# A mixture-of-experts layer: expert outputs added to the residual rows in DRAM by indirect DMAs, in place of a one-hot combination on TensorE and a sum in SBUF

## The chip, the cores and the metric

The kernel is one program on one core of a Trainium2 chip. The metric is the device time of the whole program in microseconds (us); lower is better. Before the change it is 1360.62 us, the median of three executions (1358.38 to 1361.21). The trace comes from one further execution, which took 1361.19 us and whose span, from its first to its last instruction, is 1359.3 us.

## What is computed

One layer of a transformer is applied to 512 latent and 128 context tokens of width 1024, all in float32. The first half is a normalisation, an input projection, two kinds of attention, and an output projection, added to the residual. The change is in the second half, the expert layer:

```python
def expert_choice_ffn(h, w_router, w_gate, w_up, w_down):
    aff = softmax(h @ w_router)                      # per token, over 16 experts
    gates, idx = lax.top_k(swapaxes(aff, 1, 2), cap) # each expert picks its tokens
    xe = h[idx]
    a, u = xe @ w_gate, xe @ w_up                    # 1024 x 1024 per expert
    ye = (silu(a) * u) @ w_down * gates[..., None]
    return zeros.at[idx.reshape(-1)].add(ye)         # back to the rows of the tokens

h = rms_norm(x, g_ffn) * (1.0 + scale2) + shift2
x = x + gate2 * expert_choice_ffn(h, *moe_w)
y = rms_norm(x, g_final)
```

Each of the 16 experts picks 64 of the latent tokens and 16 of the context tokens, so 80 rows per expert. scale2, shift2 and gate2 are rows of 1024 numbers, one for latent tokens and one for context tokens. A token may be picked by several experts.

## The kernel before

The work is written out by hand for the five engines, which meet only at counted semaphores. Products are made to float32 accuracy by splitting each operand into a high part (rounded to fp32r) and a low part (the rest), and multiplying high by high, high by low, and low by high.

**Weights.** Each expert has three weight matrices (gate, up, down), each cut into 8 blocks of 128x1024 values, called halves here (512 KB). A group is 4 experts, so 96 halves; there are 4 groups, 384 halves. SP loads the halves into 12 slots in turn and may load a slot again once TensorE has used it (`s_half`). ACT rounds a half to `w_hi` (L1422, 6 buffers), DVE subtracts to get the low part (`expert_lo`, L1776), and TensorE runs `half_product` (L1078 to L1080): for each of two PSUM banks three matmuls of 128x512, six matmuls a half. ACT and DVE work 4 halves ahead (`LEAD`).

**Order.** `BLOCK_ORDER` sets it: g0 u0 g1 d0 u1 g2 d1 u2 g3 d2 u3 d3 for the experts 0 to 3 of a group, 8 halves each. Every engine's group body runs through the same 96 steps, `h`. Rows of the tokens are gathered for a whole group by one-hot matmuls (`gather`, L1028 and L1029) with `sel_g` and `sel_c`, the matrices that name the token of each slot; those for the next group are put between the halves of d3 (and `sel_g` for it is made at step 40). After u come the product h_act (L2023), four transposes a half of it (`turn_hidden`, L1069), and the split of the transposed values (`hidden_hi`, `hidden_lo`).

**Outputs, which the change replaces.** The result of a down projection stands in PSUM banks 4 and 5. ACT writes it times the gate of its row to `yc_f` for context rows (L1456) and to `ye_hi` for latent rows (L1458), and DVE writes the low part `ye_lo` (L2036). Two more one-hot matrices, `sel_t` and `sel_tc`, are made by DVE (`select_slots`) from the places and affinities of the tokens, which POOL brings by broadcasting DMAs from DRAM (L2260) in each group. When the four outputs of a group are there, TensorE adds them into token order (`combine`, L1049, L1050 and L1052): for each 128 tokens and each half of the 1024 columns four matmuls of 128x512 for latent tokens, and one in full float32 for context tokens. These ten steps of a group stand behind halves 5 to 14 of the next group; DVE adds each to `acc` in SBUF (L1976). Those of the last group stand behind everything, with the end of the program.

**The end.** In group 3 POOL reloads the residual rows `x_f` (2560 KB), gate2 (1024 KB) and `g_fin` from DRAM (L2285 to L2287). After the last half, for each of 5 tiles of 128 tokens: combine, two additions to `acc` (L1976), `acc` times gate2 (L2083), plus `x_f` (L2085), the sum of squares on ACT (L1495), the reciprocal root on POOL (L2130, L2133), times it and `g_fin` (L2088), and the store by POOL (L2300).

## Time and profile before

| | |
|---|---|
| time, median of 3 runs | 1360.62 us (1358.38 to 1361.21) |
| the profiled execution | 1361.19 us, span 1359.3 us |
| TensorE (PE) busy | 1223.0 us, 90% of the span |
| VectorE (DVE) busy | 972.2 us, 72% |
| ScalarE (ACT) busy | 751.3 us, 55% |
| GpSimd (POOL) busy | 136.5 us, 10% |
| mean granted clock of TensorE | 0.964 of full speed |
| moved by DMA | 295.26 MB |
| first expert half to the last | 692.66 us to 1314.32 us of the span |

PE is TensorE's matmuls and PEld its weight loads, which run beside them. A matmul's listed duration (some 0.39 us for 128x512) is longer than the distance from one start to the next, because matmuls are pipelined: what a matmul costs is the distance between starts. A wait is put down to the instruction that released it. The granted clock 1.00 is TensorE's upper level, 2.4 GHz; the lower is 1.2 GHz, in which starts lie 0.43 us apart.

### The profile page before, as it was taken

To read this page: it belongs to the slowest core of one execution; us is meant where nothing else is said; L and a number is where in the kernel's file an instruction comes from. 1 tells how busy PE (TensorE), PEld (TensorE's weight loads), DVE (VectorE), ACT (ScalarE), POOL (GpSimd) and SP (SyncE) were. 2 spreads that over 40 slices of the span, in tenths; PEclk is the share of its full clock that TensorE was granted. 3 is DMA by queue.
4 is the path that set the end of the run, shared out by engine and by line. 5 is a ranking of instruction groups with operands and counts; after the bars stand their busy time and mean duration, and the time that the engine had idled before them with its cause. 6 is when DMAs were issued, how large, how long until landed. Compare 5 with 4: busy or idle time off the path is not lost.

```text
span 1359.3 us, 17500 instructions
## 1 busy us (share of the span) xinstructions
PE 1223.0 (90%) x6001; PEld 966.1 (71%) x6001; DVE 972.2 (72%) x1245; ACT 751.3 (55%) x1049; POOL 136.5 (10%) x210
## 2 busy tenths in 40 slices
PE   2799977988889999999399999999999999999972
PEld 0578766767767777777288888788887888678851
DVE  1754528788756232444779999999999999799956
ACT  1523236666643221223568887588776887578831
POOL 2133330000000000000620001000010000100002
PEclk9899989999989999999699999999999999999976
DMA  9642231111053343554559997899888997999901
GB/s 327 263 174 69 62 89 30 30 30 30 1 217 124 124 124 127 214 203 155 201 205 382 369 368 228 305 389 366 308 296 294 383 363 266 379 339 375 369 35 77
DMA packets 109481, 295.26 MB, mean 217 GB/s; under 512 B 29857, under 2 KB 31602, under 8 KB 108642
## 3 DMA queue, kind: packets, MB, share of 16 engines
q1 hardware_dynamic: 102802, 265.99, 54.1%
q0 software_dynamic: 6032, 19.43, 4.3%
q10 hardware_dynamic: 576, 8.91, 1.7%
q8 instruction: 43, 0.70, 0.2%
q14 instruction: 28, 0.23, 0.0%
HBM read 276.78 MB, written 12.27 MB: 213 GB/s over the span
## 4 chain that ended last, share of the span: by engine, by line
PE 77%; DVE 11%; DMA 4%; ACT 3%; issue 3%; SPq 1%; POOL 1%; DVEq 0%; ACTq 0%; POOLq 0%
PE ps L1078 12%; PE ps L1079 12%; PE ps L1080 12%; PE ps L671 9%; PE ps L672 9%; PE ps L673 9%; PE ps L863 2%; DMA raw<-in_w_mod_dram 2%; PE ps L847 2%; DVE neg_max L1686 2%; DVE raw_lo L1776 2%; DMA raw<-in_w_exp_up_dram 1%; PE ps L886 1%; PE ps L693 1%; PE ps L1049 1%
## 5 line engine op out<-in xcount | busy, mean ns | idle before, releaser
L1776 DVE TENSOR_TENSOR raw_lo<-raw,w_hi 128x1024 fp32r<-128x1024 f32 x256 | 300.9, 1217 | 33.1 <-ACT w_hi L1422 26.4
L1422 ACT ACTIVATE w_hi<-raw 128x1024 fp32r<-128x1024 f32 x252 | 259.2, 1057 | 62.0 <-PE ps L1080 58.5
L1078 PE MATMUL ps<-w_hi,xe_hi 128*128 128x512 f32 x512 | 207.6, 405 | 1.8 <-DVE xe_lo L1950 1.8
L1080 PE MATMUL ps<-w_hi,xe_lo 128*128 128x512 f32 x512 | 201.8, 394 | 0.0
L1422 ACT ACTIVATE w_hi<-extra 128x1024 fp32r<-128x1024 f32 x128 | 135.8, 1064 | 51.9 <-PE ps L1080 43.4
L1776 DVE TENSOR_TENSOR extra_lo<-extra,w_hi 128x1024 fp32r<-128x1024 f32 x128 | 151.9, 1218 | 11.2 <-ACT w_hi L1422 11.0
L671 PE MATMUL ps<-w_hi,ht_hi 128*128 128x512 f32 (+1 forms) x360 | 141.8, 394 | 12.4 <-DVE raw_lo L494 6.4
L673 PE MATMUL ps<-w_hi,ht_lo 128*128 128x512 f32 (+1 forms) x360 | 139.1, 387 | 0.0
L672 PE MATMUL ps<-raw_lo,ht_hi 128*128 128x512 f32 (+1 forms) x360 | 139.1, 386 | 0.0
L489 ACT ACTIVATE w_hi<-raw 128x1024 fp32r<-128x1024 f32 x50 | 50.8, 1054 | 134.0 <-DMA raw<-in_w_in_dram 53.9
L494 DVE TENSOR_TENSOR raw_lo<-raw,w_hi 128x1024 fp32r<-128x1024 f32 x50 | 60.2, 1229 | 88.8 <-ACT w_hi L489 88.3
L1078 PEld LDWEIGHTS ps<-w_hi,xe_hi 128*128 128x128 f32 x512 | 96.3, 188 | 25.0 <-DVE xe_lo L1950 2.0
L1079 PE MATMUL ps<-raw_lo,xe_hi 128*128 128x512 f32 x288 | 113.9, 395 | 0.0
L1080 PEld LDWEIGHTS ps<-w_hi,xe_lo 128*128 128x128 f32 x512 | 96.4, 188 | 23.5
L1078 PE MATMUL ps<-w_hi,ht_hi 128*128 128x512 f32 x256 | 102.7, 401 | 4.3 <-DVE ht_lo L2028 4.3
L1080 PE MATMUL ps<-w_hi,ht_lo 128*128 128x512 f32 x256 | 102.0, 398 | 0.0
L671 PEld LDWEIGHTS ps<-w_hi,ht_hi 128*128 128x128 f32 x360 | 68.7, 191 | 31.7 <-issue 11.8
L1079 PE MATMUL ps<-raw_lo,ht_hi 128*128 128x512 f32 x224 | 89.5, 399 | 0.0
L1079 PE MATMUL ps<-extra_lo,xe_hi 128*128 128x512 f32 x224 | 88.6, 396 | 0.0
L673 PEld LDWEIGHTS ps<-w_hi,ht_lo 128*128 128x128 f32 x360 | 68.5, 190 | 15.0
L672 PEld LDWEIGHTS ps<-raw_lo,ht_hi 128*128 128x128 f32 x360 | 68.7, 191 | 13.7
L1686 DVE TENSOR_REDUCE neg_max<-ps 128x1 f32<-128x768 f32 x64 | 58.3, 952 | 8.8 <-PE ps L847 8.4
(300 smaller groups left out, 2176.1 us busy)
## 6 DMA issues: line engine op xcount, KB each, us to landing
raw<-in_w_exp_down_dram SPq DMA_DIRECT2D x112, 512.0 KB, 5.2
raw<-in_w_exp_gate_dram SPq DMA_DIRECT2D x80, 512.0 KB, 5.6
extra<-in_w_exp_up_dram SPq DMA_DIRECT2D x64, 512.0 KB, 5.5
raw<-in_w_exp_up_dram SPq DMA_DIRECT2D x64, 512.0 KB, 6.0
raw<-in_w_mod_dram SPq DMA_DIRECT2D x24, 1024.0 KB, 8.4
extra<-in_w_exp_gate_dram SPq DMA_DIRECT2D x48, 512.0 KB, 5.5
raw<-in_w_in_dram SPq DMA_DIRECT2D x17, 1024.0 KB, 5.5
extra<-in_w_exp_down_dram SPq DMA_DIRECT2D x16, 512.0 KB, 5.0
```

Source lines behind the costliest of these rows:

```text
L489: act.activation(w_hi[:, n % NHL, :], raw_half(raw, h), ACT.Copy).then_inc(s_hi, 1)
L494: dve.tensor_tensor(raw_half(raw_lo, h), raw_half(raw, h), w_hi[:, n % NHL, :].bitcast(F32), ALU.subtract)\
L671: pe.matmul(b, stat_hi(k, tt), hi[:, kk, :], start=first, stop=False)
L672: pe.matmul(b, stat_hi(k, tt), lo[:, kk, :], start=False, stop=False)
L673: mm = pe.matmul(b, stat_lo(k, tt), hi[:, kk, :], start=False, stop=last)
L847: mm = pe.matmul(bank(bb, 0, n), q[:, m % 4, t * P:(t + 1) * P], keys_t[:, x, c0:c0 + n], start=(part == 0), stop=(part == 1))
L1078: pe.matmul(b, stat_hi, hi[:, cols], start=(k == 0), stop=False)
L1079: pe.matmul(b, stat_hi, lo[:, cols], start=False, stop=False)
L1080: mm = pe.matmul(b, stat_lo, hi[:, cols], start=False, stop=(k == KD - 1))
L1422: act.activation(w_hi[:, (DENSE_SPLITS + h) % NHL, :], expert_half(h), ACT.Copy)\
L1686: dve.tensor_reduce(nm, src[:, :, 0:384], AX.XY, ALU.max, negate=True).then_inc(s_max, 1)
L1776: dve.tensor_tensor(expert_lo_half(h), expert_half(h), w_hi[:, (DENSE_SPLITS + h) % NHL, :].bitcast(F32), ALU.subtract).then_inc(s_lo, 1)
```

## The change

The combination, its one-hot matrices, `acc`, the reload of gate2 and the broadcasts of places and affinities go. The 64 latent and 16 context rows of an expert now lie side by side (80 columns of the stationary operand in place of 128, 80 rows in PSUM). The table of affinities has one more column, the token's number. At step 10 of a group TensorE multiplies this table by `sel_g` and `sel_c` of the group (`find_rows`, 20 small float32 matmuls of 17 columns), and DVE copies from the result, at step 12, the token number of each row (`rows_e`) and its gate (`gate_e`). When a down projection is done, DVE makes `y_g`, the PSUM values times the row's gate times gate2, in one instruction (`output`), and POOL adds its 80 rows of 4 KB to the rows of `x1_dram` by an indirect DMA that accumulates (`scatter`). Each waits for the one before it to have landed. After the 16th, SP loads the 5 tiles of `x_f`, and the last normalisation follows. gate2 stays in SBUF; `xn_hi`, `xn_lo` and `x_f` move to make room, so that the third tile of `xn_lo` waits for the copy of the residual to DRAM.

```diff
+EROWS = CAPL + CAPC
...
         pos_n = sb("pos_n", [P, NT, NE])
-        gate_p = sb("gate_p", [P, 3])
         gate_e = sb("gate_e", [P, EG])
+        rows_e = sb("rows_e", [P, EG], U32)
...
-        xn_hi = at("xn_hi", 0, [P, NT, D], F32R)
-        xn_lo = at("xn_lo", 20480, [P, NT, D], F32R)
+        xn_hi = at("xn_hi", 12288, [P, NT, D], F32R)
+        xn_lo = at("xn_lo", 32768, [P, NT, D], F32R)
...
+        x1_dram = nc.dram_tensor("x1_dram", [TOK, D], F32).ap()
...
                 body(i, False)
+            sp.wait_ge(s_scat, 16 * NE)
+            for t in range(NT):
+                sp.dma_start(x_f[:, t, :], x1_dram[t * P:(t + 1) * P, :]).then_inc(s_x[t], 16)
...
-            def combine(g1, n):
-
...
+            def find_rows(i, first):
+
+                pe.wait_ge(s_ids, 1)
+                pe.wait_ge(s_selg, i * NTL + NTL)
+                pe.wait_ge(s_selc, i + 1)
+                if not first:
+                    pe.wait_ge(s_h2l, i * 8)
+                for e in range(EG):
+                    cols = (e * (NE + 1), (e + 1) * (NE + 1))
+                    for t in range(NTL):
+                        pe.matmul(bank(6, *cols, slice(0, CAPL)), sel_g[:, t, e * CAPL:(e + 1) * CAPL].bitcast(F32),
+                                  aff_n[:, t, :], start=(t == 0), stop=(t == NTL - 1))
+                    mm = pe.matmul(bank(6, *cols, slice(CAPL, EROWS)), sel_c[:, e * CAPC:(e + 1) * CAPC].bitcast(F32),
+                                   aff_n[:, NTL, :], start=True, stop=True)
+                mm.then_inc(s_slots, 1)
 
...
+                    else:
+                        pe.wait_ge(s_rows, 2 * i + 2)
                     for k in range(4):
-                        mm = pe.transpose(bank(6 + f, k * P, (k + 1) * P), h_act[:, f, k * P:(k + 1) * P], ident)
+                        mm = pe.transpose(bank(6 + f, k * P, k * P + EROWS), h_act[0:EROWS, f, k * P:(k + 1) * P],
+                                          ident[0:EROWS, 0:EROWS])
                     mm.then_inc(s_htr, 1)
...
-                        b = bank(banks + f)
+                        b = bank(banks + f, rows=slice(0, EROWS))
...
+                            w = slice(e * EROWS, (e + 1) * EROWS)
                             half_product(AT[kind, e] + k, 0 if kind == "g" else 2, xe_hi[:, k, w], xe_lo[:, k, w], k)
                         if kind == "g" and e and k in (2, 3):
                             turn_hidden(e - 1, k - 2)
-                        if not first and 5 <= AT[kind, e] + k < 5 + 2 * NT:
-                            combine(i, AT[kind, e] + k - 5)
+                        if AT[kind, e] + k == 10:
+                            find_rows(i, first)
...
-            for n in range(2 * NT):
-                combine(NG, n)
 
...
-                def output_hi(e):
-
...
-                    act.activation(ye_hi[lat, e // 2, :], ps[lat, 4 * 512:6 * 512], ACT.Identity,
-                                   scale=gate_e[lat, e:e + 1]).then_inc(s_yeh, 1)
 
...
-            def add_outputs(g1, n):
-
...
-                dve.tensor_tensor(acc[:, t, cols], acc[:, t, cols], bank(6 + n % 2), ALU.add).then_inc(s_add, 1)
...
-                def select_slots(q):
-
...
-                    dve.tensor_reduce(gate_p[:, q:q + 1], gates[:, 0:n], AX.X, ALU.add).then_inc(s_gate, 1)
...
+                def rows_of_group():
+
+                    table = bank(6, 0, EG * (NE + 1), slice(0, EROWS))
+                    dve.wait_ge(s_slots, i + 1)
+                    if not first:
+                        dve.wait_ge(s_scat, 16 * EG * i)
+                    dve.tensor_copy(rows_e[0:EROWS, :], table.rearrange("p (e c) -> p e c", e=EG)[:, :, NE])\
+                       .then_inc(s_rows, 1)
+                    dve.tensor_copy(gate_e[0:EROWS, :], table[:, bass.ds(EG * i, EG, NE + 2)]).then_inc(s_rows, 1)
...
+                def output(e):
+
+                    dve.wait_ge(s_half, i * GH + H0 + (AT["d", e] + KD if e >= 0 else 0))
+                    dve.wait_ge(s_rows, 2 * i + (2 if e >= 0 else 0))
+                    if not first or e > 1:
+                        dve.wait_ge(s_scat, 16 * (EG * i + e - 1))
+                    dve.scalar_tensor_tensor(y_g[0:EROWS, e % 2, :], ps[0:EROWS, 4 * 512:6 * 512],
+                                             gate_e[0:EROWS, e % EG:e % EG + 1], gate2[0:EROWS, :], ALU.mult, ALU.mult)\
+                       .then_inc(s_yg, 1)
 
...
-                        if not first and 6 <= h < 6 + 2 * NT:
-                            add_outputs(i, h - 6)
-                        if h in (17, 19, 28):
-                            select_slots({17: 0, 19: 2, 28: 1}[h])
-                        if h == 29:
-                            gates_of_rows()
+                        if h == 12:
+                            rows_of_group()
                         if h == 40 and not last:
                             select_group(i + 1)
...
             def finish(t):
 
-                if t < NT:
-                    dve.wait_ge(s_add, (NG - 1) * 2 * NT + 2 * t + 3)
-                    if t == 0:
-                        dve.wait_ge(s_fin, 48)
-                    dve.tensor_tensor(acc[:, t, :], acc[:, t, :], gate2_f[:, t // NTL, :], ALU.mult).then_inc(s_fg, 1)
-                    dve.wait_ge(s_fg, t + 1)
-                    dve.tensor_tensor(x_f[:, t, :], x_f[:, t, :], acc[:, t, :], ALU.add).then_inc(s_fx, 1)
-                if t:
-                    dve.wait_ge(s_frs, t)
-                    dve.scalar_tensor_tensor(x_f[:, t - 1, :], x_f[:, t - 1, :], rs[:, t - 1:t], g_fin[:, :],
-                                             ALU.mult, ALU.mult).then_inc(s_fy, 1)
+                dve.wait_ge(s_frs, t + 1)
+                if t == 0:
+                    dve.wait_ge(s_gfin, 16)
+                dve.scalar_tensor_tensor(x_f[:, t, :], x_f[:, t, :], rs[:, t:t + 1], g_fin[:, :], ALU.mult, ALU.mult)\
...
             for t in range(NT):
-                add_outputs(NG, 2 * t)
-                add_outputs(NG, 2 * t + 1)
                 finish(t)
-            finish(NT)
...
+            for v in range(2):
+                pool.dma_start(gate1[:, v, :], b_mod[:, 2 * D:3 * D].to_broadcast([P, D])).then_inc(s_gb1, 16)
+                rows = slice(64 * v, 64 * v + 64)
+                pool.dma_start(gate2[rows, :], b_mod[:, 5 * D:6 * D].to_broadcast([64, D])).then_inc(s_gb2, 16)
+            pool.iota(aff_n[:, :, NE:NE + 1].rearrange("p t c -> p (t c)"), [[P, NT]], base=0, channel_multiplier=1,
+                      allow_small_or_imprecise_dtypes=True).then_inc(s_ids, 1)
...
+                if t == 2:
+                    pool.wait_ge(s_x1out, 16)
...
-            pool.memset(xe_hi[:, :, :].bitcast(F32), 0.0).then_inc(s_pool, 1)
-            pool.wait_ge(s_pool, own())
...
-            def body(i, first, last):
-                def spread(dst, src, e, rows, cols, semaphore):
...
-            pool.wait_ge(s_g, NG * KD)
-            pool.dma_start(x_f[:, :, :], x1_dram[:, :, :]).then_inc(s_fin, 16)
-            pool.dma_start(gate2_f[:, :, :], g2_dram[:, :, :]).then_inc(s_fin, 16)
-            pool.dma_start(g_fin[:, :], g_final.rearrange("(a n) -> a n", a=1).to_broadcast([P, D]))\
-                .then_inc(s_fin, 16)
-            body(NG - 1, False, True)
+            def scatter(n):
+
+                e = n % EG
+                pool.wait_ge(s_yg, n + 1)
+                if n == 0:
+                    pool.wait_ge(s_x1out, 16)
+                else:
+                    pool.wait_ge(s_scat, 16 * n)
+                pool.indirect_dma_start(x1_dram[:, :], bass.IndirectOffsetOnAxis(ap=rows_e[0:EROWS, e:e + 1], axis=0),
+                                        y_g[0:EROWS, e % 2, :], None, compute_op=ALU.add).then_inc(s_scat, 16)
+
+            for n in range(NE):
+                if n == NE - 2:
+                    pool.wait_ge(s_g, NG * KD)
+                    pool.dma_start(g_fin[:, :], g_final.rearrange("(a n) -> a n", a=1).to_broadcast([P, D]))\
+                        .then_inc(s_gfin, 16)
+                scatter(n)
+            pool.wait_ge(s_scat, 16 * NE)
```

On TensorE, in groups 1 to 3 of before, this is what stands behind half 5, between the last rows of that half and the first of half 6 (`ye_hi`, `ye_lo` are the outputs of the group before, `sel_t` a one-hot matrix, `xe_hi` the gathered rows, `w_hi` and `raw_lo` the weights):

```order
L1080 MATMUL ps<-w_hi,xe_lo 128x512
L1038 REGISTER_ALU
L1039 ISA [waits s_yel]
L1049 MATMUL ps<-ye_hi,sel_t 128x512 [waits s_gate]
L1050 MATMUL ps<-ye_lo,sel_t 128x512
L1049 MATMUL ps<-ye_hi,sel_t 128x512
L1050 MATMUL ps<-ye_lo,sel_t 128x512
L1073 REGISTER_ALU
L1078 MATMUL ps<-w_hi,xe_hi 128x512 [waits s_lo]
L1079 MATMUL ps<-raw_lo,xe_hi 128x512
L1080 MATMUL ps<-w_hi,xe_lo 128x512
L1078 MATMUL ps<-w_hi,xe_hi 128x512
```

Now nothing stands there, and behind half 10 (the last rows of that half stand first):

```order
L1063 MATMUL ps<-extra_lo_128,xe_hi 80x512
L1064 MATMUL ps<-w_hi,xe_lo 80x512
L1032 MATMUL ps<-aff_n,sel_g 64x17 [waits s_h2l,s_selc,s_selg]
L1032 MATMUL ps<-aff_n,sel_g 64x17 x3
L1034 MATMUL ps<-aff_n,sel_c 16x17
L1032 MATMUL ps<-aff_n,sel_g 64x17 x4
L1034 MATMUL ps<-aff_n,sel_c 16x17
L1032 MATMUL ps<-aff_n,sel_g 64x17 x4
L1034 MATMUL ps<-aff_n,sel_c 16x17
L1032 MATMUL ps<-aff_n,sel_g 64x17 x4
L1034 MATMUL ps<-aff_n,sel_c 16x17
L1062 MATMUL ps<-w_hi,xe_hi 80x512 [waits s_lo]
```

The ten combinations have gone from between the halves; twenty small matmuls stand in one place in their stead, and the expert products give 80 rows.

On DVE, from the last low parts of weights on, before (`acc` is the sum in SBUF, `gate_f` the reloaded gate2):

```order
L1776 TENSOR_TENSOR extra_lo_129<-extra_127,w_hi 128x1024 [waits s_hi] x2
L2036 SCALAR_TENSOR_TENSOR ye_lo<-ps,gate_e,ye_hi 64x1024 [waits s_yeh]
L1976 TENSOR_TENSOR acc<-acc,ps 128x512 [waits s_cmb,s_add]
L1976 TENSOR_TENSOR acc<-acc,ps 128x512 [waits s_cmb]
L2083 TENSOR_TENSOR acc<-acc,gate_f 128x1024 [waits s_fin,s_add]
L2085 TENSOR_TENSOR x_f<-x_f,acc 128x1024 [waits s_fg]
L1976 TENSOR_TENSOR acc<-acc,ps 128x512 [waits s_cmb] x2
L2083 TENSOR_TENSOR acc<-acc,gate_f 128x1024 [waits s_add]
L2085 TENSOR_TENSOR x_f<-x_f,acc 128x1024 [waits s_fg]
L2088 SCALAR_TENSOR_TENSOR x_f<-x_f,rs,g_fin 128x1024 [waits s_frs]
L1976 TENSOR_TENSOR acc<-acc,ps 128x512 [waits s_cmb] x2
```

And now (`gate_94` is gate2):

```order
L1954 TENSOR_TENSOR ht_lo<-ps,ht_hi 128x320 [waits s_h2h] x2
L1734 TENSOR_TENSOR extra_lo_127<-extra_125,w_hi 128x1024 [waits s_hi]
L1734 TENSOR_TENSOR extra_lo_128<-extra_126,w_hi 128x1024 [waits s_hi] x2
L1963 SCALAR_TENSOR_TENSOR y_g<-ps,gate_e,gate_94 80x1024 [waits s_scat,s_rows,s_half]
L2005 SCALAR_TENSOR_TENSOR x_f<-x_f,rs,g_fin 128x1024 [waits s_gfin,s_frs]
L2005 SCALAR_TENSOR_TENSOR x_f<-x_f,rs,g_fin 128x1024 [waits s_frs] x4
```

DVE keeps one product after the last half and the five last scalings of the tiles; the sums, and the products with gate2, are gone. What stands between is on POOL:

```order
L2168 DMA g_fin<-in_g_final_dram 128x1024 [waits s_g]
L2162 DMA x_dram<-y_g,rows_e 640x1024 [waits s_scat,s_yg] x2
L2044 TENSOR_SCALAR rs<-ss 128x1 [waits s_fss,s_scat]
L2047 TENSOR_TENSOR rs<-rs,tab 128x1 [waits s_pool]
L2044 TENSOR_SCALAR rs<-ss 128x1 [waits s_fss]
L2047 TENSOR_TENSOR rs<-rs,tab 128x1 [waits s_pool]
L2182 DMA out_dram<-x_f 128x1024 [waits s_fy]
L2044 TENSOR_SCALAR rs<-ss 128x1 [waits s_fss]
```

There the last two scatters come behind the load of `g_fin`, and the first root behind the last scatter. On SP, at the end of the weights:

```order
L616 DMA extra_126<-in_w_exp_down_dram 128x1024 [waits s_half]
L620 REGISTER_ALU
L620 COMPARE_AND_BRANCH
L624 DMA x_f<-x_dram 128x1024 [waits s_scat]
L624 DMA x_f<-x_dram 128x1024 x4
```

The reload of the five tiles, which POOL issued as one DMA in group 3 before, now waits for the last scatter.

## Rows read from the trace of the kernel before

**Rows 1.** Busy us (instructions) by stretch: PE, PEld, DVE, ACT, POOL; clock, DMA share, GB/s.

```profile
692.66:841.04 148.38, 147.32 (x688) 120.93 (x689) 139.59 (x156) 119.00 (x129) 9.50 (x19) 1.00 0.92 340
841.04:998.57 157.53, 156.45 (x725) 127.50 (x724) 147.09 (x167) 120.33 (x130) 8.10 (x17) 1.00 0.90 329
998.57:1156.12 157.55, 156.48 (x725) 127.51 (x724) 147.09 (x167) 120.31 (x130) 10.05 (x21) 1.00 0.90 328
1156.12:1314.50 158.38, 152.43 (x645) 120.35 (x643) 132.63 (x137) 110.83 (x115) 6.29 (x13) 0.97 0.86 319
1314.50:1359.30 44.80, 15.94 (x36) 9.76 (x36) 25.85 (x26) 7.96 (x12) 8.93 (x15) 0.64 0.14 59
```

**Rows 2.** Timeline of PE in group 1: start us, duration us, engine, line, what.

```profile
850.51 0.40 PE L1078 MATMUL ps<-w_hi,xe_hi 128*128 128x512 f32 x1
...
852.84 0.39 PE L1078 MATMUL ps<-w_hi,xe_hi 128*128 128x512 f32 x1
```

**Rows 3.** Timeline early in group 3: PE, and ACT waiting (idle before, releaser).

```profile
1167.00 0.40 PE L1049 MATMUL ps<-ye_hi,sel_t 128*128 128x512 f32 x1
...
1172.92 1.06 ACT L1422 ACTIVATE w_hi<-extra 128x1024 fp32r<-128x1024 f32 x1 [2.94 <-DMA extra<-in_w_exp_up_dram]
...
1181.32 0.39 PE L1049 MATMUL ps<-ye_hi,sel_t 128*128 128x512 f32 x1
```

**Rows 4.** Timeline of DVE, then PE, ahead of the last down projection.

```profile
1289.38 2.36 DVE L1776 TENSOR_TENSOR raw_lo<-raw,w_hi 128x1024 fp32r<-128x1024 f32 x2 [1.99 <-ACT w_hi L1422]
...
1297.39 1.27 DVE L2023 TENSOR_TENSOR h_act<-h_act,ps 128x512 f32<-128x512 f32 x2
...
1295.71 0.39 PE L1080 MATMUL ps<-w_hi,xe_lo 128*128 128x512 f32 x1
...
1300.45 0.80 PE L1078 MATMUL ps<-w_hi,ht_hi 128*128 128x512 f32 x1 [1.08 <-DVE ht_lo L2028]
```

**Rows 5.** Timeline of PE in the routing: small float32 matmuls, merged.

```profile
653.88 0.64 PE L957 MATMUL ps<-x_t,router_s 128*32 128x128 f32 x16 [0.21 <-DVE x_t L1872]
654.45 1.29 PE L997 MATMUL ps<-sum_q,lg_t 128*128 128x16 f32 x10
```

**Rows 6.** Groups of weight loads: count, busy us, mean ns of one.

```profile
L882 PEld LDWEIGHTS ps<-p_t,va_n 128*64 128x64 f32 x192 | 12.4, 136 | 8.7 <-issue 4.0
...
L1078 PEld LDWEIGHTS ps<-w_hi,xe_hi 128*128 128x128 f32 x512 | 96.3, 188 | 25.0 <-DVE xe_lo L1950 2.0
```

**Rows 7.** Timeline of the end of the program.

```profile
1314.09 0.40 PE L1080 MATMUL ps<-w_hi,ht_lo 128*128 128x512 f32 x1
...
1316.80 1.29 DVE L2036 SCALAR_TENSOR_TENSOR ye_lo<-ps,gate_e,ye_hi 64x1024 fp32r<-64x1024 f32 x1 [8.44 <-ACT ye_hi L1458]
...
1326.45 1.22 POOL L2130 TENSOR_SCALAR rs<-ss 128x1 f32<-128x1 f32 x1 [125.72 <-ACT squares L1495]
1327.76 1.57 POOL L2133 TENSOR_TENSOR rs<-rs,tab 128x1 f32<-128x1 f32 x1
...
1345.46 0.18 POOL L2130 TENSOR_SCALAR rs<-ss 128x1 f32<-128x1 f32 x1 [3.52 <-ACT squares L1495]
1345.73 0.56 POOL L2133 TENSOR_TENSOR rs<-rs,tab 128x1 f32<-128x1 f32 x1
...
1347.91 0.53 POOL L2300 DMA_DIRECT2D out_dram<-x_f  x1 [1.06 <-DVE x_f L2088]
```

**Rows 8.** Groups of instructions in the whole program: busy us, mean ns of one.

```profile
L2088 DVE SCALAR_TENSOR_TENSOR x_f<-x_f,rs,g_fin 128x1024 f32<-128x1024 f32 x5 | 6.4, 1280 | 1.4 <-POOL rs L2133 1.4
L1495 ACT ACTIVATE squares<-x_f 128x1024 f32<-128x1024 f32 x5 | 5.3, 1058 | 22.9 <-DVE x_f L2085 22.9
```

**Rows 9.** DMA issues: count, KB each, median us from issue to landing.

```profile
extra<-in_w_exp_up_dram SPq DMA_DIRECT2D x64, 512.0 KB, 5.5
...
x_dram<-x_r ACTq DMA_DIRECT2D x1, 2560.0 KB, 9.0
...
out_dram<-x_f POOLq DMA_DIRECT2D x5, 512.0 KB, 2.9
```

248 lines of the change are left out of this document (59 added, 189 removed).

## Prediction

> **What bounds the kernel now.** I read the busy time by stretch first, cut at the first half of each group. In groups 0 to 2 TensorE is busy in all but 1.1 us of each stretch at granted clock 1.00 [rows 1], and the chain of waits is a chain of its matmuls there. So a group lasts as long as the distances between the starts of its matmuls. The timeline gives that distance: ten starts (four of a combination, six of a half) take 852.84 - 850.51 = 2.33 us [rows 2], 0.233 each, whatever the listed 0.39 says. Group 0 has no combination and lasts 148.38 us; groups 1 and 2 have one, otherwise the same work, and last 157.53 and 157.55 [rows 1]. DVE is close behind with 139.6 to 147.1 us a group, and the DMA queues are busy for 0.90 to 0.92 of the time. Group 3 has no gathers and still lasts 158.38 us: it holds two stalls, below. The end, from the last half at 1314.32 (1314.09 plus one distance) to the last store's issue at 1347.91 [rows 7], is 33.6 us with TensorE mostly idle; another 11.4 us follow to the end of the span, which I leave as they are.
>
> **The change part by part.** The sum is made against the profiled execution, 1361.19 us, 0.6 above the median of the three runs.
>
> Combination between the halves. It costs 157.53 - 148.38 = 9.15 and 157.55 - 148.38 = 9.17 us in groups 1 and 2 [rows 1]; group 3 runs the same one. Gone: 3 x 9.16 = **-27.5**. The additions to `acc` and the making of `sel_t` on DVE, and the two evacuations of every expert on ACT, lay beside TensorE and count for nothing by themselves.
>
> Late weights in group 3. The reload of `x_f`, gate2 and `g_fin` falls into its start. ACT waits up to 2.94 us for a half, and TensorE needs 1181.32 - 1167.00 = 14.3 us for four rounds of ten starts that are worth 9.3 [rows 3], part of it at the lower clock. After the change only `g_fin` (512 KB, as one half) is loaded in group 3, and late. **-5.0**.
>
> The stall ahead of the last down projection. TensorE's last matmul of u3 ends its turn at 1295.94 (1295.71 + 0.23), but DVE comes to `h_act` only at 1297.39, because it stood for 1.99 us behind ACT, which was evacuating d2 [rows 4]. ACT no longer does that, so DVE is there 1.4 us sooner: **-1.4**. The rest of the stall, to 1300.45, and the slow matmuls after it stay: the chain h_act, transposes, split is as long as before. If the clock doesn't fall there, some 2 us more go; I don't count on it.
>
> `find_rows`. It adds 20 float32 matmuls a group, seen twice each as every float32 matmul is (L997: five in the code, x10), so 40. The trace has no 64x17. From below: 16 with 32 stationary columns take 0.64 us, less the 0.28 that the last one takes, 0.024 each [rows 5]: 1.0 us a group. From above: 10 with 128 stationary columns take 1.29 us, 0.114 each: 4.6 us. The table's 64 columns are half of 128, so I take about half of 4.6: 2.5 us, nearer the second row in shape (16 columns streamed). Four times: **+10.0** (4.0 to 18.4). It waits for nothing late: `sel_g` was made at step 40 of the group before. DVE's `rows_of_group` at step 12 waits for it, with the low parts of later halves queued behind; but DVE has by then prepared up to half 16, so TensorE has five halves, 7 us, in hand.
>
> Narrower operands. Half matmuls still stream 512 columns, so I give them the same 0.233. The transposes and their split get a little cheaper: zero.
>
> Before the groups. POOL's memsets go; they ran beside DVE's top-k, which ends the routing. The wait of the third tile of `xn_lo` for the copy of the residual to DRAM is covered: the copy lands in 9.0 us [rows 9], and POOL has two tiles to do first. Zero.
>
> Scatters beside the weights. Fifteen of them run in the groups, 328 KB each, written once and read once. A group then moves 96 x 0.524 + 4 x 0.66 = 52.9 MB in 150.9 us, 351 GB/s, against 340 at a share of 0.92 in group 0 [rows 1]: a share of 0.95. Zero, as long as a scatter takes little more than its bytes. DVE's `output` waits for the scatter two experts back, over 30 us old, and its next row table at step 12 for the last scatter of the group before, issued around step 1: 11 halves of 1.4 us, 15 us, to land. Zero.
>
> The end. Before, 33.6 us. Now, from 1314.32: DVE's product with its start 1.6 us (the same shape took 1.29 [rows 7]); POOL's issue of the last scatter, 1.1 (a plain one takes 0.53; with row numbers more, up to 3); its landing. Landing of 512 KB in a quiet queue is 2.9 us, a 2560 KB copy into this very tensor 9.0 [rows 9]; I take 2.9 and half as much again for the read ahead of the write, **4.4**, as it is nearest to the small one. Then the first 512 KB tile: 3.4 (2.9 quiet, 5.5 in the full queue [rows 9]). ACT 1.25 (1.06 and its accumulator), POOL's first root 3.0 (1326.45 to 1329.33, the slow first one [rows 7]). Then POOL sets the pace: a root (1345.46 to 1346.29, with its start 0.75) and an issue (0.6) per tile, four times, and one DVE product of 1.3 [rows 8]: 6.75. Sum 21.5, so **-12.1**.
>
> The Trainium skill, DMA: Bandwidth & Descriptors, section Anatomy of one DMA, gives about 2.0 us plus bytes over 436 GB/s for a DMA issued by GpSimd, 2.8 us for a scatter (an estimate), silent on accumulation. By it the end would be 1.6 us shorter and the sum 1323.6. No row here shows an accumulating DMA.
>
> Sum: -27.5 - 5.0 - 1.4 + 10.0 - 12.1 = -36.0. 1361.19 - 36.0 = **1325.2 us**. Its own range: `find_rows` -6 or +8.4; the end -2.5 (landing 2.9, issue and load at their lowest) or +8.6 (landing 9.0, issue 3, load 5.5); the clock -2; small waits at the new semaphores +3: 1314 to 1345.
>
> **The rivals.**
>
> Slower: the scatters hold the queues. If a row that is read, added and written occupies a DMA engine while it does so, the weights behind it come late, as in group 3 [rows 3]. At a share of 1 the queues would move 340/0.92 = 370 GB/s, so the weights of a group need 136 us and leave 15, 3.7 us for each of four scatters. From there each us costs 4 us a group, 16 in all; at 6 us a scatter the whole gain of 36 us is gone. At 7 us, not far from the 9.0 of the large copy: 4 x (136 + 28 - 150.9) = 52, so 1377 us. For it speaks that the share is near 1 already; against it that 328 KB is small, and that five rows per engine can overlap. The Trainium skill, same page, section SWDGE vs HWDGE vs iDMA, has each DMA engine take turns between GpSimd's and the hardware's queues, which would let a slow scatter delay weights but not block them; no run here shows it.
>
> Faster, but less: the scatters are light but slow to land, 20 us under load (long issue on POOL beside a busy DVE). Then DVE stands 4.6 us at the table of groups 1 to 3, 14 us, and the end grows by the 15.6 beyond 4.4: 1355 us. The largest landing in rows 9, 9.0, speaks against it.
>
> Faster still: the 80-column loads shorten the halves. 512 columns at 2.4 GHz are 0.213 us; the distance is 0.233. If the 0.020 were the load's and went with its columns, 48/128 of it on 2304 matmuls saves 17 us: 1308. Against it, a load of 0.188 fits inside 0.233 already. Loads do shrink: 136 ns for 64 columns, 188 for 128 [rows 6]. The Trainium skill, TensorE: Matmul & The Clock Gate, section LDWEIGHTS, states that a load takes time by its columns; the rows agree.
>
> **How the numbers follow.** Forecast 0.73; narrower loads 0.08; slow landing 0.07; held queues 0.09; some other loss that leaves the time within 0.2% 0.03. A measurement of this kernel can tell 0.2%, 2.7 us, from no change. So faster 0.73 + 0.08 + 0.07 = 0.88, same 0.03, slower 0.09. The range takes in the forecast's own bounds and the narrower loads, 1307 to 1346, and leaves out 0.07 + 0.09 + 0.03 = 0.19.
>
> **What would show it.** Right: every group from 0 to 2 near 151 us with TensorE busy throughout and starts 0.233 apart; `find_rows` 2 to 3 us; no wait of ACT for weights; scatters landing in 4 to 9 us; the end some 33 us from the last half to the span's end. Wrong: waits of ACT for DMA behind each scatter (held queues), DVE idle at `rows_e` on the scatter (slow landing), starts under 0.23 apart (loads), or a gap of over 10 us between the last `y_g` and the first square.

## The result, and the profile after

The changed kernel takes 1318.62 us (median of four executions, 1314.15 to 1322.01) against 1359.50 us for the kernel before (1357.19 to 1361.21): ratio 0.9698, 95% interval 0.9658 to 0.9739. The forecast was 1325.2, range 1307 to 1346. The profiled execution took 1315.43 us, span 1313.6, which is 45.8 us less than the profiled one before, where the sum had 36.0. Direction and range hold, but the sum is 10 us short, and the runs below look for that.

The changed kernel by the same stretches as rows 1, first half of each group to the next, then the end: length, busy us of PE, PEld, DVE, ACT, POOL, clock, DMA share, GB/s.

```profile
692.49:840.57 148.08, 148.08 (x729) 99.63 (x729) 135.26 (x142) 112.71 (x122) 16.86 (x3) 1.00 0.92 340
840.57:990.43 149.86, 149.78 (x730) 100.40 (x728) 136.10 (x142) 111.70 (x121) 22.18 (x4) 0.99 0.95 345
990.43:1141.69 151.26, 148.79 (x729) 99.31 (x728) 134.63 (x143) 111.68 (x121) 32.40 (x4) 1.00 0.93 342
1141.69:1284.50 142.81, 140.83 (x649) 90.56 (x647) 121.62 (x114) 102.30 (x107) 22.88 (x5) 0.99 0.89 330
1284.50:1313.60 29.10, 0.00 (x0) 0.00 (x0) 7.70 (x6) 5.75 (x10) 9.89 (x16) 0.58 0.54 192
```

Less [rows 1], line by line, with what the sum had for it in brackets: -0.3 (+2.5), -7.7 (-6.7), -6.3 (-6.7), -15.6 (-13.1), -15.7 (-12.1). TensorE is busy throughout groups 0 and 1, which still makes the distance between its starts the price of everything. Group 2 holds waits of 2.5 us.

TensorE around `find_rows` in group 1 (start us, duration, engine, line, what; the products come as four such pairs of rows):

```profile
855.69 0.40 PE L1064 MATMUL ps<-w_hi,xe_lo 128*80 128x512 f32 x1
856.01 0.64 PE L1032 MATMUL ps<-aff_n,sel_g 128*64 128x17 f32 x8
856.58 0.22 PE L1034 MATMUL ps<-aff_n,sel_c 128*16 128x17 f32 x2
...
858.88 0.62 PE L1062 MATMUL ps<-w_hi,xe_hi 128*80 128x512 f32 x1
859.29 0.63 PE L1063 MATMUL ps<-extra_lo,xe_hi 128*80 128x512 f32 x1
...
862.28 0.47 PE L1064 MATMUL ps<-w_hi,xe_lo 128*80 128x512 f32 x1
862.59 0.39 PE L1062 MATMUL ps<-w_hi,xe_hi 128*80 128x512 f32 x1
```

From the start of the last product ahead, 855.69, to the first one behind, 858.88, are 3.19 us; less the 0.23 that this product takes anyway, `find_rows` costs 2.96 us, the same in all four groups. Behind it nine starts lie up to 0.43 apart, the distance of 1.2 GHz (the granted clock from 858.88 to 862.28 is 0.52): 1.6 us more, in this group alone.

Group 2, DVE, then POOL, then TensorE's two waits:

```profile
993.60 2.36 DVE L1734 TENSOR_TENSOR raw_lo<-raw,w_hi 128x1024 fp32r<-128x1024 f32 x2 [3.22 <-ACT w_hi L1400]
998.28 1.28 DVE L1963 SCALAR_TENSOR_TENSOR y_g<-ps,gate_e,gate 80x1024 f32<-80x1024 f32 x1 [2.32 <-issue]
...
1006.29 5.75 DVE L1734 TENSOR_TENSOR raw_lo<-raw,w_hi 128x1024 fp32r<-128x1024 f32 x5
1018.37 0.16 DVE L1941 CAST rows_e<-ps 80x4 uint32<-80x4 f32 x1 [6.33 <-DMA x_dram<-y_g,rows_e]
...
999.84 13.49 POOL L2162 DMA_INDIRECT x_dram<-y_g,rows_e  x1 [32.40 <-DVE y_g L1963]
...
998.59 0.40 PE L1064 MATMUL ps<-w_hi,xe_lo 128*80 128x512 f32 x1
1000.75 0.46 PE L1062 MATMUL ps<-w_hi,xe_hi 128*80 128x512 f32 x1 [1.76 <-DVE raw_lo L1734]
...
1018.84 0.40 PE L1064 MATMUL ps<-w_hi,xe_lo 128*80 128x512 f32 x1
1019.89 0.46 PE L1062 MATMUL ps<-w_hi,xe_hi 128*80 128x512 f32 x1 [0.65 <-DVE raw_lo L1734]
```

DVE stands still twice early in the group: 3.22 us ahead of 993.60 (counting the halves in order, the `w_hi` that it needs there was ready at 990.31, so ACT, which the row names, is not the cause), then 2.32 us with no releaser. It catches up back to back to 1012.0, and the scatter's issue, which began meanwhile, takes 13.49 us, to 1013.3, where most take 5.5. Then DVE waits 6.33 us for that scatter to land. This wait is the slow-landing rival, in one group instead of three. TensorE loses 2.8 us over its usual distance in this group: 1.9 at 1000.75, which is DVE's own standing still and not the scatter's doing, and 0.8 at 1019.89, behind the scatter. ACT's waits for weights are all but gone (1.3 us in the four groups, 10.9 before): nothing of the held queues is there. The scatters' landings, 5.0 to 18.5 us after the start of the issue, median 11.9, are far from the 4 to 9 us that were to be seen.

The end (POOL, SP, ACT and DVE, to be held against [rows 7, 8]):

```profile
1284.50 1.28 DVE L1963 SCALAR_TENSOR_TENSOR y_g<-ps,gate_e,gate 80x1024 f32<-80x1024 f32 x1 [5.90 <-PE ps L1064]
1286.06 1.40 POOL L2162 DMA_INDIRECT x_dram<-y_g,rows_e  x1 [18.93 <-DVE y_g L1963]
1291.07 2.37 SPq L624 DMA_DIRECT2D x_f<-x_dram  x5
1294.29 1.06 ACT L1453 ACTIVATE squares<-x_f 128x1024 f32<-128x1024 f32 x1 [16.94 <-DMA x_f<-x_dram]
1295.61 0.19 POOL L2044 TENSOR_SCALAR rs<-ss 128x1 f32<-128x1 f32 x1 [8.14 <-ACT squares L1453]
...
1302.53 1.28 DVE L2005 SCALAR_TENSOR_TENSOR x_f<-x_f,rs,g_fin 128x1024 f32<-128x1024 f32 x1 [0.73 <-POOL rs L2047]
1303.13 0.74 POOL L2044 TENSOR_SCALAR rs<-ss 128x1 f32<-128x1 f32 x1
1303.95 0.56 POOL L2047 TENSOR_TENSOR rs<-rs,tab 128x1 f32<-128x1 f32 x1
1304.47 0.60 POOL L2182 DMA_DIRECT2D out_dram<-x_f  x1
1304.55 1.29 DVE L2005 SCALAR_TENSOR_TENSOR x_f<-x_f,rs,g_fin 128x1024 f32<-128x1024 f32 x1 [0.73 <-POOL rs L2047]
1306.13 0.53 POOL L2182 DMA_DIRECT2D out_dram<-x_f  x1 [1.06 <-DVE x_f L2005]
```

Issue and landing of the last scatter take 5.0 us together (5.5 in the sum), the first tile 3.2 (3.4), the first root 0.85 (3.0), and the tiles come 2.0 us apart (1.35). The last store is issued 21.8 us behind the last half (its end, 1284.30, taken as in the sum), but only 7.5 us follow, not 11.4. The view of the program's closing instructions tells why, for the kernel before and then for the changed one (line, engine's sequencer, count, ns, start):

```profile
L212 POOLq DRAIN  x1: 8065/8065/8065, 1351.0 to 1351.0; - x1
```

```profile
L205 POOLq DRAIN  x1: 3825/3825/3825, 1309.2 to 1309.2; - x1
```

The last store lands 2.9 us behind its issue in both kernels. Behind it POOL runs one closing instruction, DRAIN, of 8.07 us in the kernel before and 3.83 in the changed one, and the span ends within 0.6 us of its end.

### The profile page after: what moved, and what is told of

Its sections match the earlier page's. It is cut to its first block, busy times and chain, and to the rows that moved or that the text cites. A ratio compares the mean times of both kernels' runs of the same rounds, so it can differ in the third digit from the quotient of the medians.

```text
span 1313.6 us, 17235 instructions
## 1 busy us (share of the span) xinstructions
PE 1180.9 (90%) x6017; PEld 848.6 (65%) x6017; DVE 913.5 (70%) x1137; ACT 717.0 (55%) x1013; POOL 185.7 (14%) x154
## 4 chain that ended last, share of the span: by engine, by line
PE 80%; DVE 8%; DMA 6%; ACT 2%; issue 2%; POOL 1%; SPq 1%; DVEq 0%; ACTq 0%; POOLq 0%
PE ps L1062 13%; PE ps L1063 13%; PE ps L1064 13%; PE ps L654 9%; PE ps L655 9%; PE ps L656 9%; PE ps L852 2%; DMA raw<-in_w_mod_dram 2%; PE ps L836 2%; DVE neg_max L1644 2%; DMA x_dram<-y_g,rows_e 2%; PE ps L875 1%; PE ps L676 1%; PE ps L1017 1%; PE ps L1018 1%
## 5 line engine op out<-in xcount | busy, mean ns | idle before, releaser
L1062 PE MATMUL ps<-w_hi,xe_hi 128*80 128x512 f32 x512 | 203.6, 398 | 4.2 <-DVE raw_lo L1734 2.4
L1064 PE MATMUL ps<-w_hi,xe_lo 128*80 128x512 f32 x512 | 202.1, 395 | 0.0
L2162 POOL DMA_INDIRECT x_dram<-y_g,rows_e x16 | 95.1, 5942 | 519.8 <-DVE y_g L1963 519.8
L1063 PE MATMUL ps<-raw_lo,xe_hi 128*80 128x512 f32 x288 | 113.5, 394 | 0.0
L1062 PEld LDWEIGHTS ps<-w_hi,xe_hi 128*80 128x80 f32 x512 | 76.0, 148 | 45.9 <-DVE raw_lo L1734 3.4
L1064 PEld LDWEIGHTS ps<-w_hi,xe_lo 128*80 128x80 f32 x512 | 76.0, 148 | 43.0 <-issue 0.5
L1062 PE MATMUL ps<-w_hi,ht_hi 128*80 128x512 f32 x256 | 101.5, 396 | 1.2 <-DVE ht_lo L1954 1.0
L1064 PE MATMUL ps<-w_hi,ht_lo 128*80 128x512 f32 x256 | 101.4, 396 | 0.0
L1063 PE MATMUL ps<-raw_lo,ht_hi 128*80 128x512 f32 x224 | 88.8, 396 | 0.0
L1063 PE MATMUL ps<-extra_lo,xe_hi 128*80 128x512 f32 x224 | 88.5, 395 | 0.0
```

The source lines that it names most:

```text
L1062: pe.matmul(b, stat_hi, hi[:, cols], start=(k == 0), stop=False)
L1063: pe.matmul(b, stat_hi, lo[:, cols], start=False, stop=False)
L1064: mm = pe.matmul(b, stat_lo, hi[:, cols], start=False, stop=(k == KD - 1))
L2162: pool.indirect_dma_start(x1_dram[:, :], bass.IndirectOffsetOnAxis(ap=rows_e[0:EROWS, e:e + 1], axis=0), y_g[0:EROWS, e % 2, :], None, com ...
```

## The experiments

Each changes the changed kernel unless it says otherwise. Its time is the median of its executions, with the ratio to the kernel before measured beside it and the 95% interval. Since an execution can differ by 6 us from the next ahead of the groups (see the end), single terms are read from the stretches of the traces.

### The combination and the reload (the kernel before, one part taken away)

`no_combine`:

```diff
-                        if not first and 5 <= AT[kind, e] + k < 5 + 2 * NT:
-                            combine(i, AT[kind, e] + k - 5)
...
-                        if not first and 6 <= h < 6 + 2 * NT:
-                            add_outputs(i, h - 6)
```

> The kernel before without the combination and the sums between the halves of groups 1 to 3: only the last group's outputs are added, at the end (three quarters of the experts' outputs are left out). Theory (the combination costs PE 9.16 us a group and nothing else hangs on it): groups 1 and 2 take 148.4 us, the profiled time is 1361 - 27.5 = 1334. Rival (part of it was hidden, other waits come in its place): groups above 150 us, time 1340 or more. The wait of PE for DVE's ht_lo ahead of each group's last down product (1.06 us), which is there in the first group too, should stay.

1336.25 us, ratio 0.9799 (0.9770 to 0.9828). Groups 1 and 2:

```profile
841.26:989.55 148.29, 147.22 (x689) 120.83 (x688) 140.45 (x157) 120.40 (x130) 8.12 (x17) 1.00 0.93 348
989.55:1137.86 148.31, 147.23 (x689) 120.83 (x688) 140.45 (x157) 120.29 (x130) 10.08 (x21) 1.00 0.93 348
```

The combination is worth 9.24 us in each of these groups, as the sum had it. In group 3 the late weights now cost 3.0 us more (138.2 us to the last down product, against 144.33 - 9.16), so the two terms aren't independent: the combination gives its full 9.2 us in group 3 only if the reload is out of the way. The wait for `ht_lo` stayed, 1.07 us.

`late_reload`:

```diff
             pool.wait_ge(s_g, NG * KD)
+            body(NG - 1, False, True)
+            pool.wait_ge(s_half, DENSE_HALVES + NG * GH - 12)
             pool.dma_start(x_f[:, :, :], x1_dram[:, :, :]).then_inc(s_fin, 16)
...
-            body(NG - 1, False, True)
```

> The kernel before with the reload of x_f, gate2 and g_final asked for 12 halves ahead of the end instead of at the start of the last group. Theory (the reload keeps the weights back 5.0 us in the last group): PE's wait near 1169 and the clock's fall after it go, the last group is 5 us shorter, the end stays as it was, 1356. Rival (the weights are late there whatever else is loaded): last group unchanged, 1361; or the end has to wait for the reload, 1361 and above.

1354.88 us, ratio 0.9932 (0.9905 to 0.9959). Group 3 to the last half:

```profile
1157.03:1309.12 152.09, 148.94 (x645) 118.81 (x643) 132.41 (x137) 111.03 (x115) 8.06 (x16) 0.99 0.90 334
```

From the same start to the last half's end it was 158.20 before ([rows 1] cuts 0.18 us later), so the reload cost 6.1 us: 5.05 ahead of the last down product, the rest in the slow matmuls behind it, of which 7 are left where there were 13.

### The width of the operands

`wide_all` has 128 rows and columns again; `wide_loads` is the same without the last pair.

```diff
-        ht2_hi = at("ht2_hi", 96256, [P, KD, EROWS], F32R)
+        ht2_hi = at("ht2_hi", 96256, [P, KD, P], F32R)
...
-                            w = slice(e * EROWS, (e + 1) * EROWS)
+                            w = slice(e * EROWS, e * EROWS + (P if e < EG - 1 else EROWS))
...
-                        mm = pe.transpose(bank(6 + f, k * P, k * P + EROWS), h_act[0:EROWS, f, k * P:(k + 1) * P],
-                                          ident[0:EROWS, 0:EROWS])
+                        mm = pe.transpose(bank(6 + f, k * P, (k + 1) * P), h_act[:, f, k * P:(k + 1) * P], ident)
```

> The changed kernel with its operands 128 wide again: hidden rows transposed 128 at a time, stationary tiles of 128 columns in all down products and in the gate and up products of three experts of four (expert 3 of a group keeps 80). Theory (narrow operands gave what the sum left out): the first group, 148.08 us in the changed kernel, goes back to about 150.9, all four groups together lose 11 us, and the profiled time is 1315.4 + 11 = 1326. Rival (the groups gained because ACT and DVE have less to do, the width of operands is free): every group within 0.5 us of the changed kernel's, time 1315 to 1318.

> As wide_all, but the transposes stay 80 rows by 80 columns; only the stationary tiles of the products (and the evacuation of the transposed rows) are 128 wide. Theory: the distance between product starts goes from 0.2313 back to 0.2327 us, 2304 starts x 5/6 x 0.0014 = 2.7 us, so 1318; the other 8 us of the gain lie in the 32 turns of hidden rows and stay. Rival: the width of the loads carries the most of it, 1325.

1321.43 us, 0.9702 (0.9685 to 0.9718), and 1319.26 us, 0.9698 (0.9682 to 0.9714). Group 0 of `wide_all`, then of `wide_loads`:

```profile
693.57:843.67 150.10, 150.10 (x729) 119.71 (x730) 136.74 (x142) 114.04 (x122) 16.86 (x3) 1.00 0.92 335
```

```profile
692.19:841.46 149.27, 149.17 (x729) 118.66 (x729) 136.46 (x142) 113.97 (x122) 16.87 (x3) 1.00 0.92 336
```

Against 148.08 the loads give 1.19 us in group 0 and the transposes 0.83; four groups make 8.1 us, where the expectation had 11. Both theories were off: it is about half the loads', half the transposes'. The traces of the kernel before and of the changed one say the same when the distances between starts in group 0 are added up by kind: the half products take 1.13 us less in the changed kernel, and the transposes 0.99 less. The mean distance between full-speed starts is 0.2327 us before, 0.2325 and 0.2324 in these two runs and 0.2313 in the changed kernel. The transposes of group 0, before and changed (count, busy us, mean ns):

```profile
L1069 PE MATMUL ps<-tab,h_act 128*128 128x128 f32 x32 | 4.6, 272 | 0.0
```

```profile
L1052 PE MATMUL ps<-tab,h_act 80*128 80x80 f32 x32 | 3.4, 232 | 0.0
```

That the profiled execution of `wide_all`, 1325.0 us, comes near the 1326 of its expectation is luck: in its group 2 TensorE has gaps of 3.6 us of the kind told of below under `unrolled` and `best`, which the widths don't explain.

What `wide_all` does not give back, 1.0 to 1.2 us a group, is the wait ahead of the group's last down product [rows 4 show the one of group 3]: the gap there was 1.34 to 1.36 us in groups 0 to 2, and is 0.19, 0.36 and 0.34 (0.12 in group 0 of `wide_all`), while `no_combine` kept it. DVE comes to `h_act` in time now. That its selections and low parts for the old combination made it late is argued, not tested.

### The scatter's issue, and the stall in group 2

`dve_busy`, behind the last `y_g` (`BUSY` is 8):

```diff
+                    for n in range(BUSY):
...
+                        dve.tensor_tensor(w_hi[:, 2 + n % 2, :], w_hi[:, 0, :].bitcast(F32),
+                                          w_hi[:, 1, :].bitcast(F32), ALU.subtract).then_inc(s_idle, 1)
```

> The changed kernel with eight subtractions of 128 x 1024 on DVE, back to back, right behind the last expert's y_g; nothing waits for them. Theory (POOL can only issue the accumulating indirect DMA in DVE's pauses): the last scatter's issue, 1.40 us in the changed kernel, ends only when the eight are done, 9.6 us or more, and the time is 1315.4 + 8 = 1324. Rival (the 5.5 to 13.5 us of the issues in the groups come from the weights' DMAs or from memory): the issue stays at 1.4 us and the time at 1315 to 1316.

1324.58 us, 0.9719 (0.9691 to 0.9748). DVE and POOL:

```profile
1284.50 9.16 DVE L2003 TENSOR_TENSOR w_hi<-w_hi 128x1024 fp32r<-128x1024 f32 x8
1284.86 10.08 POOL L2168 DMA_INDIRECT x_dram<-y_g,rows_e  x1 [18.93 <-DVE y_g L1964]
```

The issue, 1.40 us beside an idle DVE, takes 10.08, to 1.3 us past DVE's last operation. The weights' DMAs were over by then. So a busy DVE is enough to hold the issue back.

`unrolled`, for DVE alone:

```diff
+            if unrolled:
+                for i in range(1, NG - 1):
+                    body(i, False, False)
...
-            groups(dve, body)
+            groups(dve, body, True)
```

> The changed kernel with DVE's program for the two middle groups written out instead of looped. Theory (DVE stood 1.9 and 2.3 us early in the third group because the loop's first return had to fetch its instructions while the weights filled the DMA engines): both gaps go, the third group takes 148.1 instead of 151.3 us, its scatter is issued in 5.5 instead of 13.5 us, time 1312. Rival (the gaps come from the fetches whatever their order, or from something else): a gap of 2 us or more remains in some group, time 1315 or above.

1313.83 us, 0.9658 (0.9634 to 0.9682). The same place in group 2:

```profile
994.31 1.27 DVE L1967 SCALAR_TENSOR_TENSOR y_g<-ps,gate_e,gate 80x1024 f32<-80x1024 f32 x1
995.86 5.55 POOL L2166 DMA_INDIRECT x_dram<-y_g,rows_e  x1 [26.88 <-DVE y_g L1967]
```

The gaps are gone, the issue takes 5.55 us, and group 2 takes 149.76 us, 148.15 without a fall of the clock behind `find_rows` that came there in this execution. The times of the expectation, 1.9 and 2.3 us, should have been 3.2 and 2.3.

The DMA view has transfers of the kind `instruction`. For the changed kernel from 985 to 1005 us, around DVE's two gaps (queue, packets, MB, share):

```profile
q14 instruction: 3, 0.02, 0.5%
```

They start at 991.2, 996.3 and 1001.1 us. `unrolled` has none at this place.

`rows16`:

```diff
-                        dve.wait_ge(s_scat, 16 * EG * i)
-                    dve.tensor_copy(rows_e[0:EROWS, :], table.rearrange("p (e c) -> p e c", e=EG)[:, :, NE])\
+                    dve.tensor_copy(rows_e[0:EROWS, bass.ds(EG * i, EG)], table.rearrange("p (e c) -> p e c", e=EG)[:, :, NE])\
```

> The changed kernel with row numbers kept for all 16 experts in columns of their own, so that DVE's copy of a group's numbers no longer waits for the last scatter of the group before. Theory (a scatter that is late holds DVE, which holds PE): DVE's wait of 6.3 us for the scatter in the third group goes, PE loses 0.65 us less there, the profiled time is 1314 to 1315, and the executions near 1322 don't appear any more if that wait is what makes them. Rival (the wait is behind enough work already done): 1315.4 and 1322 both appear as before.

1316.81 us, 0.9667 (0.9649 to 0.9685), four executions from 1314.05 to 1318.41. The issue still took 13.49 us, but nobody waited for it, and group 2 took 150.27 us, 1.0 less: that is what the late scatter cost. The two gaps of DVE and TensorE's first wait stayed, as they should. The expectation of 1314 to 1315 for the profiled execution failed: it took 1318.41, since it came to the groups at 698.1 instead of 692.5. None of its executions is near 1322, but `written_out` below, without this wait too, still has executions 6 us apart, so the wait is not what makes them.

`plain` leaves `compute_op=ALU.add` out of the scatter.

> The changed kernel with scatters that overwrite the rows instead of adding to them (the residual and all but the last expert's output of a row are left out). Theory (the landing of 5.0 us at the end is the read and write back of the rows by the accumulation): the last scatter lands in 3 us or less, the time is 2 us shorter. Rival (it is what the software-built descriptors cost): 5 us stay, and the issue of 5.5 us in the groups too.

1313.52 us, 0.9656 (0.9629 to 0.9682). The last scatter lands 3.3 us after the start of its issue instead of 5.0, and the issue takes 0.91 instead of 1.40; in the groups it takes 5.05 instead of 5.55 (medians). So adding costs 1.7 us, 0.5 of it in the issue, and the long issues are not its doing. The 3 us or less of the expectation were not reached; the times of the two kernels scatter too much to show its 2 us.

### The clock behind find_rows, and the end

`spread` has both edits above, and:

```diff
-                        if AT[kind, e] + k == 10:
-                            find_rows(i, first)
+                        if 9 <= AT[kind, e] + k < 9 + EG:
+                            find_rows(i, first, AT[kind, e] + k - 9)
```

> The changed kernel with three edits: DVE's groups written out (as unrolled), row numbers for all experts (as rows16), and find_rows cut into one expert's products behind each of four halves instead of four experts' behind one. Theory (2.7 us of small products in one piece make the clock fall to 1.2 GHz for 3.4 us right behind them in one to two of the four groups, at 1.6 us each): no fall behind find_rows in any group, groups 0, 1 and 2 take 148.1 us each, time 1311 to 1312. Rival (the clock falls whatever the pieces): falls stay, groups of 149.7 us, 1313 to 1315.

1317.69 us, 0.9684 (0.9664 to 0.9703), above the 1311 to 1312 of the expectation; profiled 1312.18. Groups 1 and 2:

```profile
840.84:989.45 148.61, 148.61 (x729) 99.35 (x728) 136.33 (x143) 111.71 (x121) 22.18 (x4) 1.00 0.95 349
989.45:1138.07 148.62, 148.62 (x729) 99.36 (x728) 136.32 (x143) 111.70 (x121) 22.18 (x4) 1.00 0.95 348
```

These groups were expected at 148.1. No fall of the clock behind the pieces, nor in `best` and `written_out`, which keep them: twelve groups without one. The eight traces with `find_rows` in one piece (the changed kernel and seven of these) each show one or two falls of 3.4 us right behind it, 11 in 32 groups. But four changes between kinds of product cost 0.4 us a group more, so that 1.6 us are paid for what one or two falls of 1.6 cost: a steadier time, not a better one.

`sp_stores` is `rows16` with the stores on SP:

```diff
+            for t in range(NT):
+                sp.wait_ge(s_fy, t + 1)
+                sp.dma_start(ys[t] if t < NTL else y_prompt[0], x_f[:, t, :]).then_inc(s_sout, 16)
```

> rows16 with the five output tiles stored by SP's queue instead of POOL's. Theory (POOL with its two root operations and a store's issue sets the 2.0 us between tiles at the end): the distance falls to 1.3 to 1.5 us, the last store is issued some 2.4 us earlier, 1312 to 1313. Rival (loads and stores of 5.2 MB share the DMA engines, 12.2 us at 430 GB/s from the first load on): tiles come 2 us apart as before, time as rows16.

1313.99 us, 0.9628 (0.9583 to 0.9673). POOL and DVE near the end:

```profile
1303.88 1.29 DVE L2008 SCALAR_TENSOR_TENSOR x_f<-x_f,rs,g_fin 128x1024 f32<-128x1024 f32 x1 [0.72 <-POOL rs L2050]
1303.93 1.29 POOL L2047 TENSOR_SCALAR rs<-ss 128x1 f32<-128x1 f32 x1
1305.30 0.55 POOL L2050 TENSOR_TENSOR rs<-rs,tab 128x1 f32<-128x1 f32 x1
1305.88 1.28 DVE L2008 SCALAR_TENSOR_TENSOR x_f<-x_f,rs,g_fin 128x1024 f32<-128x1024 f32 x1 [0.72 <-POOL rs L2050]
```

The theory failed: the tiles come 2.0 us apart without the issues too. POOL's operation on 128 numbers, 0.19 us beside an idle DVE, ends with DVE's scaling of the tile before, and its `pow` follows: 1.28 + 0.72. The rival isn't right either, since the gain came elsewhere: from the last scaling's end to the span's end are 3.0 us instead of 7.7, and from the start of the last `y_g` 24.3 instead of 29.1. POOL's DRAIN still takes 3.86 us, but it runs from 1305.4 to 1309.3, beside SP's last stores; the last of these lands at 1309.8, and the program ends at 1310.2.

`best` is `spread` and `sp_stores` together, with the root on ACT and DVE:

```diff
+                act.activation(rs[:, t:t + 1], ss[:, t:t + 1], ACT.Sqrt, scale=1.0 / D, bias=eps).then_inc(s_frs, 1)
...
+                dve.reciprocal(rs[:, t:t + 1], rs[:, t:t + 1]).then_inc(s_root, 1)
```

> spread, with the output tiles stored by SP's queue, and the root of the mean taken by ACT (Sqrt) and DVE (reciprocal) instead of POOL. Theory (POOL's scalar operation can't end while DVE scales a tile, so tiles come 1.28 + 0.73 us apart whoever stores them): the distance falls from 2.0 to 1.5 us, the last store is issued 2 us earlier than in sp_stores counted from the last half, and from there to the end it is 3 us as there; together 24.5 - 2 = 22.5 us from the last half to the end, time 1304 to 1306. Rival (loads and stores share the DMA engines, or a table load on ACT and the small operations take what POOL's took): the distance stays at 1.9 us or more and the time is 1307 to 1308.

1312.32 us, 0.9629 (0.9602 to 0.9656), executions from 1306.04 to 1316.91; the 1304 to 1306 of the expectation was missed. Tiles now come 1.4 us apart, but the third waits for its load, and the end takes 23.3 us from the last `y_g` on, 1.0 less than in `sp_stores`. The profiled execution had its first expert half at 698.2 and two gaps in group 2:

```profile
996.65 0.40 PE L1075 MATMUL ps<-w_hi,ht_lo 128*80 128x512 f32 x1
998.06 0.45 PE L1073 MATMUL ps<-w_hi,xe_hi 128*80 128x512 f32 x1 [1.01 <-DVE raw_lo L1746]
...
1000.65 0.39 PE L1075 MATMUL ps<-w_hi,xe_lo 128*80 128x512 f32 x1
1002.92 0.47 PE L1073 MATMUL ps<-w_hi,xe_hi 128*80 128x512 f32 x1 [1.88 <-DVE raw_lo L1746]
```

DVE had no gap and prepares four halves ahead, so the named releaser is not the cause. TensorE went back to the start of its loop at 992.8 us, four us ahead of the first gap, and here, too, instructions are moved, on another queue than in the changed kernel (990 to 1008 us; they start at 993.0, 995.3 and 1000.7):

```profile
q8 instruction: 3, 0.05, 1.1%
```

`written_out`:

```diff
-            groups(pe, body)
+            groups(pe, body, True)
...
-            groups(act, body)
+            groups(act, body, True)
```

> best with the groups written out on TensorE and ACT too, not on DVE alone. Theory (in the third group of best TensorE stood 1.2 and 2.0 us at its own loop's first return, as DVE did in the changed kernel; what is written out has no return): all groups take 148.5 us, the stretch from the last half to the end 21.8 us as in best, and the time is 1303 to 1304 where the front part takes 692 us and 1309 to 1310 where it takes 698. Rival (the wait for instructions comes wherever the weights fill the DMA engines, loop or not): a gap of 2 us or more in some group, as in best.

1306.83 us, 0.9635 (0.9608 to 0.9661), the lowest median of all; by their ratios `sp_stores`, `best` and this one can't be told apart. Executions 1306.4, 1306.7, 1306.8, 1312.8 and 1313.3. Groups 0 to 2 take 148.5 us each without a gap, as expected. The end is 23.1 us, much as in `best`: the 21.8 of the expectation was counted from the scatter's issue, 1.6 us later, my slip, and makes up 1.6 of the 3 us by which its time was too low.

## Why the prediction was right, and where it was short

**Combination**, -27.5: measured 3 x 9.24 = 27.7, group 3 taken like groups 1 and 2. Right.

**Late weights**, -5.0: 6.1 (`late_reload`). Right in kind; the slow matmuls behind the last down product were partly the reload's too.

**Stall ahead of the last down projection**, -1.4: from u3's last matmul to the first of d3 it went from 4.74 us [rows 4] to 3.30. Right. That the same lateness cost 1.0 to 1.2 us in each of groups 0 to 2 was in no step: -3.2. It stood in [rows 1], as the 1.1 us of each stretch in which TensorE is not busy.

**find_rows**, +10.0: 4 x 2.96 = +11.9, within its 4.0 to 18.4. Its fall of the clock, +1.6, was missed.

**Narrower operands**, 0: this is the step that failed. "I give them the same 0.233" should have been 0.231, and the transposes were not free: 2.1 us a group, 1.1 of them by the loads and 1.0 by the transposes, -8.5 in all. What remains of group 0 agrees (148.38 + 2.96 - 1.15 - 148.08 = 2.1). The rival of narrower loads had the mechanism of one half of this, at a quarter of its 17 us (4.5); nobody had the other half.

**Scatters beside the weights**, 0: the scatters themselves cost 0.8 to 1.0 us, by the late landing in group 2. Another 1.9 us there is DVE standing still, which is no term of the prediction: +2.8 together. The rival of slow landing had DVE's wait for the row table about right (6.3 us for its 4.6, in one group), but put all of it on TensorE, which had halves in hand.

**The end**, -12.1: -15.7. Up to the last store's issue it was right (21.8 us for 21.5) by cancelling errors, the first root (3.0 for 0.85) against four tiles at 2.0 for 1.35 (in the rows read, a root took 0.83 us, where the sum put 0.75). "I leave as they are" for the 11.4 us behind the last issue missed 3.9, which is POOL's closing DRAIN. Why it got shorter is open: POOL issues 98 DMAs in the kernel before and 46 in the changed one, but 41 in `sp_stores` with a DRAIN as long as with 46.

Together: -27.7 - 6.1 - 1.4 - 3.2 + 11.9 + 1.6 - 8.5 + 2.8 - 15.7 = -46.3, against -45.7 of the spans; the 0.6 us between them belong to no term. So the sum of -36.0 lacked 16.6 us of gains and 6.3 us of losses; that it was only 10 us short is in part luck.

Of the signs that were to tell right from wrong, two would have misled. The starts did not come under 0.23 us apart (0.2313), though the loads were at work. And landings of 12 us, outside the 4 to 9, cost next to nothing.

## What to carry to other kernels

Where TensorE is busy throughout, look at the distance between starts for every edit that narrows a stationary operand: 0.0014 us on thousands of matmuls is a term, and count the transposes. An operation put on POOL is not free time beside a busy DVE: ask whether DVE pauses. Look at what follows the last store: if it is POOL's closing DRAIN, let another engine's queue (here SP's) make the last stores, so that the DRAIN runs beside them.
